# Delta rule: decay matrix built on VectorE and ScalarE in place of two TensorE products

## What is computed

```python
gc = jnp.cumsum(chunks(g), axis=-1)            # running sums of the log decays
diff = gc[..., :, None] - gc[..., None, :]
decay = jnp.where(tri, jnp.exp(jnp.where(tri, diff, 0.0)), 0.0)
m = jnp.where(strict, jnp.einsum('nbhik,nbhjk->nbhij', kb, kc) * decay, 0.0)
sol = lax.linalg.triangular_solve(m + eye, rhs, left_side=True, lower=True, unit_diagonal=True)
qk = jnp.where(tri, jnp.einsum('nbhik,nbhjk->nbhij', qc, kc) * decay, 0.0)
qg = qc * jnp.exp(gc)[..., None]
# per chunk: v_new = u - w s;  o = qg s + qk v_new;  s = s * exp(gc_last) + kg^T v_new
```

## Time and profile before

| | us |
|---|---|
| median of 3 runs | 4269.63 (4269.42 to 4272.04) |
| the profiled execution, first to last instruction | 4269.3 |
| PE busy in it | 3984.7 (93%) |
| DVE, ACT, POOL busy | 2371.6, 1526.6, 781.1 |

### The profile page before, as it was taken

How to read it: one execution, slowest core, us unless ns; L and a number is a source line. 1 busy time by engine, 2 the same in 40 slices (tenths; PEclk the granted TensorE clock), 3 DMA queues, 4 the chain that set the end, 5 groups by cost and what they waited for, 6 DMA issues and landing times. The chain is left out here.

```text
span 4269.3 us, 57778 instructions
## 1 busy us (share of the span) xinstructions
PE 3984.7 (93%) x20052; PEld 3058.8 (72%) x20052; DVE 2371.6 (56%) x3119; ACT 1526.6 (36%) x2467; POOL 781.1 (18%) x698
## 2 busy tenths in 40 slices
PE   8999999999989999998999999999059999999998
PEld 3444446456769999998778778788048888888886
DVE  5555420355646666665443434344876777777674
ACT  5333311225642222222342424222124444444442
POOL 3877100011113333332000000000100010100000
PEclk9999999999989999999999999999579999999999
DMA  7334241011131222221534434243147676667663
GB/s 300 89 108 120 63 126 34 16 54 40 24 139 60 76 85 75 74 74 65 185 101 166 159 104 155 85 155 138 74 133 219 215 214 210 215 206 216 205 218 94
DMA packets 234600, 542.97 MB, mean 127 GB/s; under 512 B 35163, under 2 KB 95867, under 8 KB 231803
## 3 DMA queue, kind: packets, MB, share of 16 engines
q1 hardware_dynamic: 202380, 426.69, 30.9%
q0 software_dynamic: 32112, 114.84, 9.1%
HBM read 439.95 MB, written 99.55 MB: 126 GB/s over the span
## 5 line engine op out<-in xcount | busy, mean ns | idle before, releaser
L2684 DVE TENSOR_TENSOR sb_we_low<-sb_we,sb_we_high 128x1024 fp32r<-128x1024 f32 x377 | 458.4, 1223 | 127.3 <-ACT sb_we_high L2636 127.2
L2636 ACT ACTIVATE sb_we_high<-sb_we 128x1024 fp32r<-128x1024 f32 x377 | 392.2, 1048 | 147.8 <-PE ey L2611 147.8
L307 PE MATMUL p_ps<-sb_hT,sb_ring 128*128 128x512 f32 (+1 forms) x960 | 379.5, 553 | 1.8 <-ACT sb_raw L450 1.8
L2114 DVE TENSOR_TENSOR sb_wm_low<-sb_wm,sb_wm_high 128x1024 fp32r<-128x1024 f32 x127 | 155.4, 1224 | 402.0 <-ACT sb_wm_high L2027 402.0
L2593 PE MATMUL eg<-sb_xe_parts,sb_we_high 128*128 128x512 f32 x1024 | 370.9, 395 | 1.6 <-DVE sb_xe_parts L2679 1.6
L2593 PE MATMUL eu<-sb_xe_parts,sb_we_high 128*128 128x512 f32 x1024 | 370.9, 394 | 0.0
L307 PEld LDWEIGHTS p_ps<-sb_hT,sb_ring 128*128 128x128 f32 x960 | 184.0, 192 | 189.2 <-issue 180.9
L1969 PE MATMUL pg<-sb_hb_high,sb_wm_high 128*128 128x512 f32 x768 | 304.2, 396 | 9.4 <-DVEq L2086 5.4
L1970 PE MATMUL pg<-sb_hb_low,sb_wm_high 128*128 128x512 f32 x768 | 300.8, 392 | 0.0
L1971 PE MATMUL pg<-sb_hb_high,sb_wm_low 128*128 128x512 f32 x768 | 300.6, 391 | 0.0
L2592 PE MATMUL eu<-sb_xe_parts,sb_we_low 128*128 128x256 f32 x896 | 251.7, 281 | 0.0
(11 more groups left out here) (411 smaller groups left out, 8549.8 us busy)
## 6 DMA issues: line engine op xcount, KB each, us to landing
sb_we<-in_w_ex SPq DMA_DIRECT2D x384, 512.0 KB, 4.4
sb_wm<-in_w_gates SPq DMA_DIRECT2D x96, 512.0 KB, 3.6
sb_wrow<-in_w_mod_row POOLq DMA_DIRECT2D x64, 256.0 KB, 3.5
sb_wm<-in_w_br SPq DMA_DIRECT2D x32, 512.0 KB, 4.4
sb_ring<-in_w_ch POOLq DMA_DIRECT2D x19, 512.0 KB, 3.6
sb_eg<-eg_d SPq DMA_DIRECT2D x36, 256.0 KB, 4.0
sb_lk<-k_d SPq DMA_DIRECT2D x36, 256.0 KB, 4.5
sb_lq<-q_d SPq DMA_DIRECT2D x36, 256.0 KB, 4.8
```

What stands on the lines that cost most here:

```text
L307: last = nc.tensor.matmul(ps[:, b % BANKS, 0:wd], w[:, kind, k], g.hT[:, k, t0:t0 + wd], start=(k == 0), stop=(k == KD - 1))
L2114: v.tensor_tensor(wl[n], w[n], wh[n], ALU.subtract).then_inc(s.wl, 1)
L2636: nc.scalar.activation(wh[:, n % CUT], w[:, n % RAW], ACT.Copy).then_inc(s.wh, 1)
L2684: v.tensor_tensor(wl[:, n % CUT], w[:, n % RAW], wh[:, n % CUT], ALU.subtract).then_inc(s.wl, 1)
```

## The change

The decay matrix no longer goes through PE. The running sums themselves are kept: ACT copies them (`g.gsums`, per position) where it took their exponent before, and the tensor that is turned and stored to memory holds running sums (`gc_d`) instead of their exponents. In `delta_rule` the broadcast load brings the row of running sums `gr`. DVE forms `dec` = row minus column (`difference`, after update 1), takes the minimum with `bar`, which is 0 inside the triangle and -1e30 outside (`clamp`, after update 2). ACT takes the exponent of `dec` in place (after `partial` 3) and, new, the exponent of the row, `eg` (`row_decays`, after `partial` 4), since no DMA brings it any more. POOL no longer forms `sb`, and waits for `eg` before `ke`. DVE forms `dq` = `dec` times beta. The split of the log decays (one ACT and one DVE instruction in the mixer) goes too.

```diff
-                        if (n, b) == (NZ, 2):
-                            act.wait_ge(sd.own, 27)
-                            a(g.gdh, gdf, ACT.Copy).then_inc(sd.gh, 1)
...
-                                for j, to in enumerate((g.egc[:, d], g.esb[:, d])):
-                                    a(to, pdec[:, 2 * d + j].rearrange("p (n h) -> p n h", h=H), ACT.Exp).then_inc(sd.ex, 1)
+                                for j, (to, func) in enumerate(((g.gsums[:, d], ACT.Copy), (g.esb[:, d], ACT.Exp))):
+                                    a(to, pdec[:, 2 * d + j].rearrange("p (n h) -> p n h", h=H), func).then_inc(sd.ex, 1)
...
-                    dve.wait_ge(sd.gh, 1)
-                    own.done(v.tensor_tensor(g.gdl, gdf, g.gdh, ALU.subtract))
...
-                    sp.dma_start(eg[d][u][:], g.eg_d[d, at].partition_broadcast(P)).then_inc(sem, 16)
+                    sp.dma_start(gr[d][u][:], g.gc_d[d, at].partition_broadcast(P)).then_inc(sem, 16)
...
-                    wait(pool, q.dq, n)
-                    tt(sb[d][:], heads(g.dirt(d, 0)), col(g.beta, d, at), ALU.mult).then_inc(q.sb, 1)
                     loaded(pool, d, n, u)
+                    pool.wait_ge(q.eg, n + 1)
                     wait(pool, q.ks, n)
                     tt(ke[d][:], lk[d][u][:], eg[d][u][:], ALU.mult).then_inc(q.ke, 1)
...
-                    act.wait_ge(q.mat, n + 1)
-                    wait(act, q.dq, n)
-                    a(dec[d][:], D_[:], ACT.Exp).then_inc(q.exp, 1)
+                    act.wait_ge(q.cl, n + 1)
+                    a(dec[d][:], dec[d][:], ACT.Exp).then_inc(q.exp, 1)
+
+                def row_decays(d, n, u):
+                    loaded(act, d, n, u)
+                    a(eg[d][u][:], gr[d][u][:], ACT.Exp).then_inc(s[d].eg, 1)
...
                     partial(d, n, 4)
+                    if new:
+                        row_decays(*new)
                     partial(d, n, 5)
...
-                def exponents(d, n, u):
-                    q, (A, B, C_, D_) = s[d], bank[d]
-                    pe.wait_ge(q.gt, 2 * n + 2)
-                    wait(pe, q.vn, n)
-                    mm(flat(D_), after[:, d], flat(gh[d]), start=True, stop=False)
-                    mm(flat(D_), after[:, d], flat(gl[d]), start=False, stop=True).then_inc(q.mat, 1)
...
                         keys(*new, (3,))
-                        exponents(*new)
                     first(d, n, u, 4)
...
-                def gate(part, d, n, u):
+                def difference(d, n, u):
 
                     at = place(nc.vector, d, n)
-                    v.tensor_tensor((gh, gl)[part][d][:], heads(g.dirt(d, 0)), col((g.gdh, g.gdl)[part], d, at),
-                                    ALU.mult).then_inc(s[d].gt, 1)
+                    loaded(dve, d, n, u)
+                    wait(dve, s[d].dq, n)
+                    v.tensor_tensor(dec[d][:], gr[d][u][:], col(g.gsums, d, at), ALU.subtract).then_inc(s[d].df, 1)
+
+                def clamp(d, n, u):
+
+                    dve.wait_ge(s[d].df, n + 1)
+                    dve.wait_ge(s[d].bar, 1)
+                    v.tensor_tensor(dec[d][:], dec[d][:], heads(bar[:, d]), ALU.min).then_inc(s[d].cl, 1)
...
-                    dve.wait_ge(q.sb, n + 1)
                     wait(dve, q.qkv, n)
-                    v.tensor_tensor(dq[d][:], dec[d][:], sb[d][:], ALU.mult).then_inc(q.dq, 1)
+                    v.tensor_tensor(dq[d][:], dec[d][:], col(g.beta, d, at), ALU.mult).then_inc(q.dq, 1)
...
                     update(d, n, u, 1)
                     if new:
-                        gate(0, *new)
+                        difference(*new)
                     update(d, n, u, 2)
                     if new:
-                        gate(1, *new)
+                        clamp(*new)
```

More of the change, by code:

```diff
@@ L709, in mixer @@
         sm = sems(nc, c, "mi", "wt blk blkc ev evc z0 z1 tok vcp acp sq sum root rec nrm v")
-        sd = sems(nc, c, "de", "par ea ay beta own sum ex gh tr row st")
+        sd = sems(nc, c, "de", "par ea ay beta own sum ex tr row st")
         sa = sems(nc, c, "at", "pad z rp sk bt0 qb sc cx add mx nm ex rc tp ptd pta o oe ot ote st0 st1")
@@ L773, in _ @@
                 sp.wait_ge(sd.row, 1)
-                sp.dma_start(g.eg_d.rearrange("d n h p -> (n h) d p"), erow).then_inc(sd.st, 16)
+                sp.dma_start(g.gc_d.rearrange("d n h p -> (n h) d p"), erow).then_inc(sd.st, 16)
                 sp.wait_ge(sd.st, 16)
@@ L874, in decay_turn @@
                     for d in range(2):
-                        last = nc.tensor.transpose(pdt[:, d * P:(d + 1) * P], g.egc[:, d].rearrange("p n h -> p (n h)"), g.ident)
+                        last = nc.tensor.transpose(pdt[:, d * P:(d + 1) * P], g.gsums[:, d].rearrange("p n h -> p (n h)"), g.ident)
                     last.then_inc(sd.tr, 1)
@@ L1311, in four @@
             return [[sbuf(nc, c, f"{name}{d}{u}", [P, H, P]) for u in range(2)] for d in range(2)]
-        lq, lk, lkt, lvt, eg, um, ob = map(four, ("lq", "lk", "lkt", "lvt", "eg", "um", "ob"))
+        lq, lk, lkt, lvt, gr, um, ob = map(four, ("lq", "lk", "lkt", "lvt", "gr", "um", "ob"))
         dec, vn, qr, mn = map(two, ("dec", "vn", "qr", "mn"))
-        gh, gl = two("gth", F32R), two("gtl", F32R)
-        sb, dq, mt, tm, qk, qg, ke, kg, rb, st = map(two, ("sb", "dq", "mt", "tm", "qk", "qg", "ke", "kgd", "rb", "st"))
+        eg = four("eg")
+        dq, mt, tm, qk, qg, ke, kg, rb, st = map(two, ("dq", "mt", "tm", "qk", "qg", "ke", "kgd", "rb", "st"))
         pm = [sbuf(nc, c, f"pm{d}", [P, H * HALF + WIDE - HALF]) for d in range(2)]
-        after = sbuf(nc, c, "after", [P, 2, P], F32R)
+        bar = sbuf(nc, c, "bar", [P, 2, P])
         bank = [[psum(nc, c, f"dr{d}{b}", (P, H, P)) for b in "abcd"] for d in range(2)]
-        names = ("ld0 ld1 gt mat exp sb dq kk mt qkp qkr qkv t0 me u0 vt pb pe pc vu t5 t5e um ke kg qg "
-                 "ks r vp vn op su sup oe st0 st1 z aft held").split()
+        names = ("ld0 ld1 df cl exp eg dq kk mt qkp qkr qkv t0 me u0 vt pb pe pc vu t5 t5e um ke kg qg "
+                 "ks r vp vn op su sup oe st0 st1 z bar held").split()
         s = [sems(nc, c, f"dr{d}", " ".join(names)) for d in range(2)]
@@ L1524, in _ @@
                 act.wait_ge(g.tail.st, 32)
+                row_decays(0, 0, 0)
                 exponent(0, 0, 0)
@@ L1692, in _ @@
                 every = range(H)
-                for d in range(2):
-                    pe.wait_ge(s[d].aft, 1)
-                exponents(0, 0, 0)
                 keys(0, 0, 0, every)
@@ L1730, in matrix @@
                     q, (A, B, C_, D_) = s[d], bank[d]
+                    at = place(nc.vector, d, n)
                     dve.wait_ge(q.exp, n + 1)
-                    dve.wait_ge(q.sb, n + 1)
                     wait(dve, q.qkv, n)
-                    v.tensor_tensor(dq[d][:], dec[d][:], sb[d][:], ALU.mult).then_inc(q.dq, 1)
+                    v.tensor_tensor(dq[d][:], dec[d][:], col(g.beta, d, at), ALU.mult).then_inc(q.dq, 1)
                     dve.wait_ge(q.dq, n + 1)
@@ L1792, in _ @@
                 for d in range(2):
-                    v.tensor_copy(after[:, d], g.dirt(d, 1)).then_inc(s[d].aft, 1)
-                for part in range(2):
-                    gate(part, 0, 0, 0)
+                    v.tensor_scalar(bar[:, d], g.dirt(d, 0), -1.0, -NEG, ALU.add, ALU.mult).then_inc(s[d].bar, 1)
+                difference(0, 0, 0)
+                clamp(0, 0, 0)
                 matrix(0, 0, 0)
@@ L2856 @@
     "o_d": (2, POS, P, H, P),
-    "eg_d": (2, POS, H, P),
+    "gc_d": (2, POS, H, P),
 }
@@ L2871, in program @@
         g.level = lambda d, lev: consts[:, C_LEV + (d * N_LEV + lev) * P:C_LEV + (d * N_LEV + lev + 1) * P]
-        g.beta, g.egc, g.esb, g.gdl = (sbuf(nc, c, n, [P, 2, POS, H])[:] for n in ("beta", "egc", "esb", "gdl"))
-        g.gdh = sbuf(nc, c, "gdh", [P, 2, POS, H], F32R)[:]
+        g.beta, g.gsums, g.esb = (sbuf(nc, c, n, [P, 2, POS, H])[:] for n in ("beta", "gsums", "esb"))
         g.ab = sbuf(nc, c, "ab", [P, NT, 16])[:]
```

## The result

The changed kernel takes 4277.1 us (median of 15 runs, 4273.7 to 4282.6) against 4269.6 (15 runs, 4266.6 to 4276.2): ratio 1.0019, 95% interval 1.0012 to 1.0026, 7.5 us slower. That is inside the range (4264 to 4279) and 7.0 above the forecast of 4270.1. The point lies within the 0.2% taken as "same"; the interval reaches past it, so slower by a little more is not excluded, and faster is.

A forecast was written before the change was run, and what follows sets the result against it. It took a ring (PE `first`, ACT copy, PE `second`, DVE update) to pace the delta rule, with PE's other matmuls in its gaps. 36 x 0.00 + 1.0 - 0.5 = +0.5 on 4269.63 gave 4270.1; range 4264 to 4279.

The forecast's parts named there:

- the two products: PE's two removed matmuls ahead of `first` 4 only fill a wait for update 3: gain 0.00 a half, bounds 0 and 0.64.
- the rival that PE's time comes out: Delta rule: the products' 0.64 us a half is real PE time, 23.0 us saved in 36 halves, 4247; chance 0.05.
- the pair's 0.64: PE time of the two products in one half, read as 1650.12 to 1650.76; 23.0 us over 36 halves.
- DVE, ACT, POOL: Steady halves: the new and moved instructions of these three engines fit into idle time; cost 0.
- the rival of the POOL chain: Steady halves: stretched POOL work pushes `begin` onto the path, 0.45 a half, 16 us slower, 4286; chance 0.08.
- the point from which it decides: Where the 0.94 idle before `rest` is used up: `begin` ending later than 1659.30, against 1658.36 before.
- The waits in the loop: PE's computed waits before `second` could spread to direction 1 or vanish: 5.6 us slower or faster; chance 0.1 together.
- the prologue: Start of the delta rule: the new chain begins only when the loads land; +0.3 to +1.5, taken as +1.0 us.
- the first half: There the products are late, so without them `first` 4 begins earlier: a gain of 0.5 us, once.
- Rival (c): PE's start-up clock: a second slow stretch costs 4.2 us, its absence gives 4266, chance 0.2; a fall in steady halves 0.02.
- (d): PE's computed waits in the loop: 5.6 us slower or faster, chance 0.1 together; 0.04 for passing 8.5 with the worst prologue.
- The upper bound: Top of the range, 4279: prologue +1.5, clock +4.2 and loop +5.6 less the 0.5, rounded down.

The follow-up runs named there:

- e8: Changed kernel with four 512-column matmuls (output unused) in each half where the two products stood; ratio 1.0024 to the kernel before, 4279.0 us.
- e6: Changed kernel with 62 semaphore increments added to PE's program ahead of a wait where PE idles anyway; ratio 1.0014 to the kernel before.
- e7: Kernel before with 194 semaphore increments added to PE's program ahead of a wait where PE idles anyway; ratio 1.0017, 4276.8 against 4270.2 us.
- e9: Changed kernel with two 512-column matmuls (output unused) in the first half alone, where the kernel before has its two products; ratio 1.0019 to the kernel before.
- e3: Changed kernel with two 512-column matmuls (output unused) once in the delta rule's prologue, before `keys`; ratio 1.0023 to the kernel before.
- e5: Changed kernel with PE's first `scores` put ahead of its first `known` in the prologue; ratio 1.0023 to the kernel before.
- e1: Changed kernel with 62 semaphore increments in PE's stage `choose`, where they turned out to lengthen PE's path; ratio 1.0029 to the kernel before.
- e4: Changed kernel with eight 512-column f32 matmuls before `keys` and stand-in matmuls in the first half (outputs unused); ratio 0.9989, 4263.1 against 4268.3 us.
- e10: e9 with 60 semaphore increments added in PE's idle time, so the expert loop lies where the kernel before has it; ratio 0.9994 to the kernel before.
- e11: Kernel before with the eight f32 matmuls before `keys` and stand-in matmuls in the first half, as in e4; ratio 0.9999 to the kernel before.
- e2: Kernel before with 194 semaphore increments in PE's stage `choose`, where they turned out to lengthen PE's path; ratio 1.0072.

## Why the prediction was right and wrong

**Right: the two products cost nothing in the steady halves.** Forecast 0.00 a half, measured -0.03 a half. `first` 4 stands 0.06 behind update 3 as before, and the idle time is where it should be. The distance between the release and the start, not PE's 97.55%, was the right row; the rival that PE's time comes out is gone. **One size in it was wrong:** the pair's 0.64 was read from the start of its first record, which overlaps the `keys` matmuls by 0.26. The pair was 0.38, and the idle time 0.38, not 0.6. At a gain of zero the error didn't count. It would have, as e8 shows, for anyone who adds work there: the spare room is 0.38, and what exceeds it comes through at 0.27 of 0.40.

**Right: DVE, ACT, POOL.** `difference` and `clamp` 0.65 each with 1.66 idle before the next update; `row_decays` hidden; `ke` at 1658.63 - 1645.94 = +12.69 (forecast +12.8), wanted by PE at 1662.51, 2.6 us after it ends (2.5). `qk` ends at +17.53 (forecast 0.08 later than today's +17.55), `begin` at +18.12, with the same 0.94 idle before `rest`. None of the three is stretched, so the rival of the POOL chain never came near the point from which it decides. The waits in the loop stayed as they were: direction 0 still 0.35 longer than direction 1.

**A term too small: the prologue.** Forecast +1.0. From the landing of the loads to the first `first` it is 1260.05 to 1267.95, 7.90, against 1261.54 to 1267.65, 6.11: +1.8. The other pair of profiles agrees (e6 7.34, e7 5.58). `ke` took 1.70, not 1.27, beside DVE's `clamp`, and `known` waited 0.50 for it; `scores` behind it take 1.77 to 1.91, on the slow clock, where e7 has 1.06. Since the loads landed 1.5 earlier, the first `first` is only 0.3 later.

**The step that failed: the first half.** The sum had -0.5 there. The 0.5 itself came, since `first` 4 starts 0.53 earlier without the products than with them (1284.06 against 1284.59 in e9) and 0.06 behind its update; but the half as a whole is 6.0 longer. The sum applied "a gap's work is worth its time only where it is longer than the gap" to a half on the slow clock. The work in that gap was also what PE had shown when its clock came back. Rival (c) had the price (4.2; the runs show 4.3 to 6.0) but as a matter of chance, at 0.2, and as either sign. It was not chance, it hung on the change: all five changed kernels without products in this half take 28.8 to 30.5, all three with them 25.4 to 25.9, the kernel before and its variant with other code 24.2 to 24.5. The row was there to be read: `first` 4 at 1.60, between 1.97 at the slow clock and 1.00 to 1.10 at the full one, said that the clock turned right behind the products. What divides after's 30.5 from the 28.8 of the others is a short return of the clock in 1265 to 1270 (0.71 to 0.84) that after's execution lacks (0.50); I have no cause for it.

**The step that was missing: the code.** The sum treated 62 instructions fewer on PE as nothing, since all of them lay in the gap. No term for where the later code lies stood in it, nor a rival. It costs 4.3 to 9.1 us in the changed kernels that have it (after, e3, e5, e9). The page of before shows 67 packets for 67.4 packets of code, and seven passes of a loop are among them: that the loop is held between passes hangs on where it lies, and this could have been a rival.

**What was luck.** That 7.5 us lay inside the range is no merit of the sum. The range was wide enough because (c) and (d) added 4.2 and 5.6 to it; (d) didn't occur, and the 4.7 of the experts stood in no term. The upper bound had a slip too: 4269.6 + 1.5 + 4.2 + 5.6 - 0.5 is 4280.4, not 4279.

## What to carry to other kernels

Work in a dependency gap is free to remove in the steady state, read by how far the next instruction stands behind its releaser; but look separately at the stretches in which TensorE's granted clock is at 0.50, since there even two matmuls that delay the ring by 0.5 us can decide how long it stays so. Whenever an edit changes the number of instructions ahead of a long loop, compare the packets of the instruction queue and the time of the loop's branch in both profiles before you explain a difference of some 0.1% by the edit itself. And a duration that a timeline shows for a group of matmuls starts under the tail of the group before: take the difference of two sizes (four products less two) or the idle time that appears.

## What the hardware showed

A loop of 1578 PE instructions (6.2 packets of 16.4 KB) is kept between its passes or fetched again by where it lies: 67 packets in the kernel before and in e1, e4, e6, e8, e10 and e11, 120 or 121 in after and in e2, e3, e5, e7 and e9. The loop's branch divides them in the same way: a median of 0.21 us in all the former, 3.7 to 4.1 in all the latter. Fetching again shows as PE's idle time by "issue", mostly 0.1 to 1 us at a time, at most 1.5 but for one wait of 2.65. It costs 0.8 us a return in after, 4.7 over six. The position at which it begins was not determined; 62 instructions decide.

The Trainium skill, page "Runtime: NRT & Kernel Launch", section "Instruction fetch mechanics", says that an engine's code is refilled in 16 KiB blocks of 256 instructions (32 KiB in all for most engines, 128 KiB or 2048 instructions for PE), and that a taken branch forces a fetch unless its target is in the current window of two pages. The block size agrees (16.4 KB, 256 instructions of 64 bytes). The window of two doesn't for PE: with 67 packets a branch back over 6.2 blocks fetched nothing in six returns. The 2048 instructions would hold this loop, but they don't say why 62 instructions ahead of it matter.

The granted clock at a stage's start followed what PE had done: 0.50 until 1292 to 1296 without products in the first half (after, e1, e3, e5, e6), until 1279 to 1286 with two or four ahead of `first` 4 (before, e2, e7 to e10), but for a short return in all of them except after, and 1.00 from 1258 or 1259 on after eight f32 products from 1253 or 1254 on (e4, e11), on a PE that would have been idle.
